# Two transformer blocks in split fp32: activations streamed as 512-wide high-and-low rows in the feed-forward up layers, 512-wide query, key and value chunks, head tiles turned amid a chunk, and bias masks built on GpSimd

## The reference, cut to what matters

```python
# first block, feed-forward of each of 2 layers (D_FF = 2816)
gt, up = jnp.split(h @ w_ffn_in[l], 2, axis=-1)
x = x + (jax.nn.silu(gt) * up) @ w_ffn_out[l]
# second block, feed-forward of each of 2 layers (4096 hidden)
#   x + gate * (relu(h @ mlp_w1)**2 @ mlp_w2)
# dilated attention: bias of a pair of tokens from a table of 32 buckets
bucket = t5_bucket(pk[:, :, None, :] - pq[:, :, :, None])
bias = jnp.moveaxis(bias_table[bucket], -1, 2).astype(jnp.float32)
# first block: q, k, v of 8 heads, width 512 each; q and k normed by head
q, k, v, ... = jnp.split(h @ w_in[l], IN_SPLITS, axis=-1)
```

## Time and profile before

| | us |
|---|---|
| median of 3 runs (1594.33 to 1598.21) | 1595.7 |
| the profiled execution's own time | 1595.42 |
| its span in the trace | 1593.6 |
| TensorE busy with matmuls | 1541.6 |
| VectorE busy | 1127.9 |
| ScalarE busy | 819.0 |
| POOL (GpSimd) busy | 130.7 |

### The profile page before, as it was taken

One profiled execution on the slowest core, in us unless ns is written; L12 is line 12 of the kernel. 1 busy time (PEld: TensorE's weight loads), 2 busy tenths in 40 slices (PEclk: granted clock), 3 DMA queues, 4 the chain that ended last, 5 costly groups with the idle time before them and its releaser, 6 DMA issues. The chain is left out here.

```text
span 1593.6 us, 27186 instructions
## 1 busy us (share of the span) xinstructions
PE 1541.6 (97%) x11270; PEld 1407.5 (88%) x11270; DVE 1127.9 (71%) x1437; ACT 819.0 (51%) x1089; POOL 130.7 (8%) x119
## 2 busy tenths in 40 slices
PE   7999999999999999999998999999999999999998
PEld 7999988999899999999987789998888888889997
DVE  6798668775679757877678666666878766765554
ACT  6564444444555444344468654445555555564442
POOL 2060000000114000000013000000201102000000
PEclk9999999999999999999999999999999999999999
DMA  9775376677676637676732357674877754355652
GB/s 305 256 239 203 128 254 204 214 239 238 224 265 228 196 107 254 226 234 214 232 120 96 95 183 246 220 253 153 306 249 270 245 185 159 121 171 174 196 185 80
DMA packets 231018, 325.44 MB, mean 204 GB/s; under 512 B 7944, under 2 KB 195824, under 8 KB 230896
## 3 DMA queue, kind: packets, MB, share of 16 engines
q1 hardware_dynamic: 223832, 313.00, 58.8%
q10 hardware_dynamic: 7064, 10.71, 2.0%
HBM read 314.23 MB, written 9.45 MB: 203 GB/s over the span
## 5 line engine op out<-in xcount | busy, mean ns | idle before, releaser
L1710 DVE TENSOR_TENSOR wparts<-raw,wparts 128x2048 fp32r<-128x2048 f32 (+1 forms) x240 | 547.1, 2283 | 223.6 <-ACT wparts L1218 223.3
L1218 ACT ACTIVATE wparts<-raw 128x2048 fp32r<-128x2048 f32 (+1 forms) x240 | 454.8, 1896 | 124.5 <-PE bank L555 84.8
L553 PE MATMUL bank<-hT,wparts 128*128 128x256 f32 x1728 | 494.0, 286 | 3.6 <-DVE hT L1831 2.1
L554 PE MATMUL bank<-hT,wparts 128*128 128x256 f32 x1728 | 488.8, 283 | 0.0
L555 PE MATMUL bank<-hT,wparts 128*128 128x256 f32 x1728 | 488.8, 283 | 0.0
L553 PEld LDWEIGHTS bank<-hT,wparts 128*128 128x128 f32 x1728 | 331.1, 192 | 10.3 <-issue 8.1
L554 PEld LDWEIGHTS bank<-hT,wparts 128*128 128x128 f32 x1728 | 331.4, 192 | 1.2
L555 PEld LDWEIGHTS bank<-hT,wparts 128*128 128x128 f32 x1728 | 331.3, 192 | 0.0
L553 PE MATMUL bank<-wparts,hT 128*128 128x256 f32 (+2 forms) x688 | 227.0, 330 | 3.9 <-DVE wparts L1710 2.1
L555 PE MATMUL bank<-wparts,hT 128*128 128x256 f32 (+2 forms) x688 | 222.1, 323 | 0.0
L554 PE MATMUL bank<-wparts,hT 128*128 128x256 f32 (+2 forms) x688 | 222.0, 323 | 0.0
(11 more groups left out here) (285 smaller groups left out, 1484.4 us busy)
## 6 DMA issues: line engine op xcount, KB each, us to landing
raw<-in_mlp_w SPq DMA_DIRECT2D x64, 1024.0 KB, 5.8
ada_raw<-in_ada_w SPq DMA_DIRECT2D x96, 512.0 KB, 6.7
raw<-in_w_ffn_in SPq DMA_DIRECT2D x44, 1024.0 KB, 5.3
raw<-in_w_in SPq DMA_DIRECT2D x43, 1024.0 KB, 5.9
raw<-in_dil_w_in SPq DMA_DIRECT2D x64, 512.0 KB, 4.7
raw<-in_w_ffn_out SPq DMA_DIRECT2D x22, 1024.0 KB, 5.1
raw<-in_w_o SPq DMA_DIRECT2D x8, 1024.0 KB, 5.4
biasb<-head_bias ACTq DMA_DIRECT2D x16, 512.0 KB, 5.6
```

Source lines behind the costliest of these rows:

```text
L553: pe.matmul(dst, held[:, 0, :], streamed[:, 0, :], start=start, stop=False)
L554: pe.matmul(dst, held[:, 0, :], streamed[:, 1, :], start=False, stop=False)
L1218: act.activation(view(whi[c % SPL], c), view(raw[c % RAW], c), ACT.Copy).then_inc(s_hi, 1)
L1710: dve.tensor_tensor(view(wlo[c % SPL], c), view(raw[c % RAW], c), view(whi[c % SPL], c).bitcast(F32), ALU.subtract).then_inc(s_lo, 1)
```

## The change

1. `hT` is laid out so that for each k the high and the low row of 256 tokens lie side by side. `hidden_slabs` takes the place of `feature_major` in GT, UP and M1: one matmul of 512 columns gives high x high in the left half of a bank and high x low in the right half, and one of 256 columns adds low x high to the right half. Each block of 128 hidden columns has its own bank, of four. ScalarE copies the right half to SBUF, VectorE adds it to the left half. SiLU, then product (now of two SBUF tiles), and ReLU with square in one instruction follow.
2. Query, key and value chunks hold half of the contraction and all 512 columns, for `wide_half`. Turns, copies and head norms follow tiles of 128 tokens.
3. In the dilated stage the second tile of a group is turned amid a chunk, not behind it; ScalarE's copy of it comes ahead of its other work of the chunk.
4. The steps and masks of the bias units move from VectorE to GpSimd (POOL). A mask is now eight instructions of 102x128, each with a per-partition scalar.

```diff
-        hT, aT = sb("hT", [P, 2, DK, S], F32R), sb("aT", [P, 2, DK, S], F32R)
+        hT_both, aT = sb("hT", [P, DK, 2, S], F32R), sb("aT", [P, 2, DK, S], F32R)
+        hT = hT_both[:, :, :, :].rearrange("p k b s -> p b k s")
...
-                for c in range(2):
-                    chunk((n, l, c), kmajor(w_in, c0 + 256 * c, 256))
+                for half in range(2):
+                    chunk((n, l, half), kmajor(w_in[512 * half:512 * half + 512], c0, DA))
...
+            def hidden_slabs(name, w, first_of=None):
+                bks = {}
+                for t, k, _, _ in block_order(2, DK, first_of):
+                    if t not in bks:
+                        bks[t] = begin("w", name + (t,), b=slab_bank())
+                    await_pair(first_of, t, k)
+                    rows = slice(P * t, P * t + P)
+                    high_and_low = hT_both[:, k, :, :].rearrange("p b s -> p (b s)")
+                    cross = bks[t][:, S:]
+                    if k < DK - 1:
+                        pe.matmul(bks[t][:, :], w[:, 0, k, rows], high_and_low, start=k == 0, stop=False)
+                        pe.matmul(cross, w[:, 1, k, rows], hT[:, 0, k, :], start=False, stop=False)
+                    else:
+                        pe.matmul(cross, w[:, 1, k, rows], hT[:, 0, k, :], start=False, stop=False)
+                        end(pe.matmul(bks[t][:, :], w[:, 0, k, rows], high_and_low, start=False, stop=True), name + (t,))
...
# TensorE, first block
-                    token_major((nm, l, c), w, 0, 256, hT, 0, DK, first_of=None if i else ("nrm", 2 * l))
+                    wide_half((nm, l), (nm, l, half), w, half, None if nm != "Q" else ("nrm", 2 * l),
+                              turn_of(i - 2) if i in (3, 5) else idle)
...
-                            feature_major((nm, l, c), w, (0, P), hT, 0, DK,
-                                          first_of=None if c or i else ("nrm", 2 * l + 1))
+                            hidden_slabs((nm, l, c), w, None if c or i else ("nrm", 2 * l + 1))
...
# TensorE, dilated stage: project
+                if m3 == 1:
+                    wide_half(("DQK", j, g), chunk_name, w, 1, ("nrm", 6) if (j, g) == (0, 0) else None, turn_next)
...
+                elif g == 1:
+                    wide_half(("DV", j), chunk_name, w, 1, between=turn_next)
...
# GpSimd, behind the norm of each feed-forward of the first block
+                pool.wait_ge(s_bits, 2 * (l + 1))
+                link(pool.tensor_copy(hi16[:, :], ihi[:, :]))
...
+                for u in range(NU):
+                    if u >= 4:
+                        full(pool, ("B", l, u - 4))
+                    k0 = unit_keys(l, u)
+                    for i in range(8):
+                        ins = pool.tensor_scalar(Gst[u % 4][:, i, :], relq[:, P * l:P * l + P], relk[:, k0 + i:k0 + i + 1], None,
+                                                 ALU.is_le)
+                    ins.then_inc(s_g, 1)
...
# ScalarE, feed-forward of the first block
+                        act.activation(crf[which == "UP"][:, t, :], bk[:, S:], ACT.Copy).then_inc(s_crossf, 1)
...
# VectorE, feed-forward of the first block
-                        dve.tensor_tensor(h32[c % 2][:, :, :], bk[:, :].rearrange("p (a s) -> p a s", a=2), sg[c % 2][:, :, :],
-                                          ALU.mult).then_inc(drain_sem(nm), 1)
+                        dve.wait_ge(s_silu, NF1 * l + c + 1)
+                        dve.tensor_tensor(h32[c % 2][:, :, :], h32[c % 2][:, :, :], sg[c % 2][:, :, :], ALU.mult)\
+                           .then_inc(s_hid32, 1)
...
+                        dve.tensor_tensor(dst[:, t, :], bk[:, 0:S], crf[which == "UP"][:, t, :], ALU.add).then_inc(drain_sem(nm), 1)
...
-                        dve.tensor_tensor(Gst[u % 4][:, :, :],
-                                          relk[:, k0:k0 + 8].unsqueeze(2).broadcast_to([NR, 8, P]),
-                                          relq[:, P * l:P * l + P].unsqueeze(1).broadcast_to([NR, 8, P]), ALU.is_ge)\
-                           .then_inc(s_g, 1)
```

More of the change, by code:

```diff
@@ L184, in block_pair @@
             sg = [sb(f"sg{i}", [P, 2, S], at=ph) for i in range(2)]
+            crf = [sb(f"crf{i}", [P, 2, S], at=ph) for i in range(2)]
             posb = sb("posb", [96, S], I32, ph)
@@ L229, in block_pair @@
             xnp = sb("xnp", [P, TT, D], at=ph)
-            rl = [sb(f"rl{i}", [P, 2, S], at=ph) for i in range(2)]
+            crm = [sb(f"crm{i}", [P, 2, S], at=ph) for i in range(2)]
             gbc2 = sb("gbc2", [P, D], at=ph)
@@ L807, in _, with gate_rows @@
                         biases(u0 + 3)
[L809 removed]
+            def gate_rows(e, col0, i, place=lambda: None):
                 pe.wait_ge(s_mods, 2 * i + (2 if col0 >= 24 else 1))
                 for half in range(2):
[L812 removed]
+                    bk = begin("w", ("gb", e, half), b=place())
                     for k in range(4):
@@ L1259, in split_half @@
             def split_half(half):
-                rows = slice(DK // 2 * half, DK // 2 * half + DK // 2)
+                rows = slice(2 * half, 2 * half + 2)
                 act.wait_ge((s_half[0], s_raw[0])[half], 16)
@@ new lines, in _ @@
+                split_ahead(("K", l, 1))
+                qk_out(0)
+                squares(2)
+                qk_out(1)
+                squares(3)
+                split_ahead(("V", l, 0))
+                act.wait_ge(s_z, l + 1)
+                link(act.activation(tf[:, :], zf[:, :], ACT.Abs))
+                act.activation(tf[:, :], tf[:, :], ACT.Exp, scale=-1.0).then_inc(s_ac, 1)
+                steps[0] += 1
+                split_ahead(("V", l, 1))
+                qk_out(2)
+                values_out(0)
@@ L1449, in stage_biases, with copy_cross @@
                         act.sem_inc(s_bst, 1)
+                def copy_cross(which, c):
+                    for t in range(2):
+                        bk = full(act, (which, l, c, t))
+                        if c:
+                            emptied(act, (which, l, c - 1, t))
+                        act.activation(crf[which == "UP"][:, t, :], bk[:, S:], ACT.Copy).then_inc(s_crossf, 1)
                 for c in range(NF1 + 1):
@@ new lines, in _ @@
+                begin_tile(3)
+                finish_head_norm()
+                bk = full(dve, ("F", l))
+                dve.tensor_scalar(zf[:, :], bk[0:H1, 0:S], fb[:, l:l + 1], None, ALU.add).then_inc(drain_sem(("F", l)), 1)
+                emptied(dve, ("F", l))
+                link(dve.memset(zero1[:, :], 0.0))
+                dve.tensor_scalar(mf[:, :], zf[:, :], 0.0, None, ALU.min).then_inc(s_z, 1)
+                split_ahead(("V", l, 0))
+                finish_head_norm()
+                split_ahead(("V", l, 1))
@@ L2168, in mlp @@
                     if c < NF2:
-                        nm = ("M1", i, c)
-                        split_ahead(nm)
-                        emptied(dve, nm)
-                        dve.tensor_tensor(h32[c % 2][:, :, :], rl[c % 2][:, :, :], rl[c % 2][:, :, :], ALU.mult)\
-                           .then_inc(s_hid32, 1)
+                        split_ahead(("M1", i, c))
+                        h = h32[c % 2]
+                        for t in range(2):
+                            nm = ("M1", i, c, t)
+                            bk = full(dve, nm)
+                            dve.wait_ge(s_crossm, 2 * (NF2 * i + c) + t + 1)
+                            dve.tensor_tensor(h[:, t, :], bk[:, 0:S], crm[c % 2][:, t, :], ALU.add).then_inc(drain_sem(nm), 1)
+                        for t in range(2):
+                            emptied(dve, ("M1", i, c, t))
+                        dve.scalar_tensor_tensor(out=h[:, :, :], in0=h[:, :, :], scalar=0.0, in1=h[:, :, :], op0=ALU.max,
+                                                 op1=ALU.mult).then_inc(s_hid32, 1)
                         dve.wait_ge(s_hidhi, 2 * NF1 + NF2 * i + c + 1)
```

239 lines of the change are left out of this document (115 added, 124 removed).

## The result

The changed kernel takes 1718.0 us (median of 4 runs, 1712.8 to 1718.4) beside 1596.5 for the kernel before (4 runs of the same session): the ratio is 1.0749, with a 95% interval of 1.0730 to 1.0768. It is 122 us slower. The forecast was 1573, with a range of 1563 to 1607.

The account below looks back on a forecast made before the run. TensorE, busy 97% of the span, was taken as the bound: 1593.6 - 15.7 - 3.7 - 4.9 - 2.7 + 5.1 = 1571.7, plus 1.8 outside the span, gave 1573 us, with a range of 1563 to 1607.

Parts of the forecast that it names:

- Part 6: Masks on POOL, block one's feed-forward: 0.28 us a piece where up to 0.27 keeps pace, costing TensorE 5.1 us.
- debt: TensorE time lost to late POOL masks: 5.1 us for each 0.01 us a piece over the pace.
- the budget: Sharing of a 17.8 us round in block one's feed-forward: VectorE takes 9.8 us, 8.0 are left for POOL.
- the gains of 27 us: Forecast savings from up layers, query/key/value chunks, dilated turns and the first mask wait, before any cost of POOL's masks.
- rival C: POOL bounds block one's feed-forward, kernel slower, above 0.333 us a piece; chance 0.27 beyond 1600.5 us, 0.05 between 1591 and 1600.5.
- Part 4: First mask of the bias units: with steps and masks on POOL, TensorE's two waits go, saving 2.7 us.
- Part 1: Up layers: a 512-wide and a 256-wide matmul replace three 256-wide, 12.9 ns less in each of 1216 blocks, 15.7 us.
- part 5: Added copies and additions for the up layers' right halves: cost nothing, covered by 10.9 us in block two.
- Parts 2 and 3: Wide query, key, value chunks save 3.7 us; earlier turns in the dilated stage remove a 4.9 us wait.

Follow-up runs that it names:

- parts 2 and 3 alone: Changed kernel with up layers as before and steps and masks on VectorE in their old place: 1589.9 us, 0.9966 of the kernel before.
- half of each mask: Changed kernel with four of each mask's eight pieces on POOL, the other four keys on VectorE: 1596.5 us, 1.0007 of the kernel before.

## Why the prediction was wrong

**Part 6, the piece, failed.** "I take 0.28, nearest in kind to the two-input rows", with 0.42 as the upper bound. Measured: 0.60 long and 0.577 apart, over the upper bound. The step behind it, "half of 2.15 for one input in place of two", was wrong in kind: the column rate is 2.5 ns, above the 2.15 of two inputs, and the fixed part 0.28 beside 0.185. The bound from above took a two-input row as the slowest that 128 columns can be, and no row of before held an instruction with a scalar. In its own sum 0.577 gives 30.7 x 5.1 = 157 us of debt and 1725, where 1718 was measured, but that nearness is luck. The masks cost 126 us, not 157, since VectorE kept 7.1 us a round from POOL and not the 9.8 less 0.7 of the budget, 32 us over 16 rounds; and the gains of 27 us that the sum takes off came to 4. VectorE's splits, which were to lengthen by 0.2 us, took 2.31 us beside 2.29 before: nearly all of the exclusion fell on POOL. So rival C held, and its condition, a piece over 0.333, was met; the chances and the end of the range rested on the wrong bound. The Trainium skill, "GPSIMD Engine Reference", section "Engine selection", calls one-input work on GpSimd roughly line-rate; by it the prediction had the piece at an estimated 0.25. The trace does not agree for the form that was needed: 0.528 with a constant, 0.603 with a scalar from SBUF; only the cast, with 0.293, came near. Its advice against moving elementwise work there held.

**Part 4 failed too.** "The wait goes": it became 8.6 us in layer 0 and 8.1 in layer 1. Masks were to begin at 233 and began at 238.46. POOL's 15 steps, put at 11 us, took 16.5 (from 221.91): five of the six on 96x256 took 1.2 to 2.6 us each beside VectorE. The first mask, eight pieces with a split and a modulation row among them, took 7.5 us more, where eight of 0.28 would be 2.2.

**Part 1 was right in kind and too large, and the rest was eaten.** Alternating widths repeat every 0.352 us in the mlp with masks on VectorE, not 0.347: the 512-wide matmul holds 235 ns, not 227, and the 256-wide one 118. The first and the sixth of six wide ones in a row of blocks:

```profile
961.22 0.40 PE L622 MATMUL bank<-hT,wparts 128*128 128x512 f32 x1
961.46 0.28 PE L623 MATMUL bank<-hT,wparts 128*128 128x256 f32 x1
...
962.98 0.40 PE L622 MATMUL bank<-hT,wparts 128*128 128x512 f32 x1
```

962.98 - 961.22 = 1.76, five times 0.352. That is 8.5 ns gained in a block of 0.360, not 12.9; in the mlp stages 256 blocks x 2 x 8.5 ns = 4.4 us, and the table says 4.2. With widths in runs the mlp stages gain 5.7. In the feed-forward of block one 704 x 8.5 ns = 6.0 us ought to come and the stages get 5.4 us longer than with parts 2 and 3 alone (207.3 + 205.5 against 203.9 + 203.5). The account against the kernel with parts 2 and 3 alone: the wait for the first masks is 7.0 us, not 3.4; 2.3 us are waited for the additions of the right halves (`sg`), which hold a bank; and 10.2 us more ran at half clock around those waits, which by the columns that TensorE streamed in it cost an estimated 4.4 us. 3.6 + 2.3 + 4.4 - 6.0 = 4.3 of the 5.4. TensorE comes to unit 0 at the same time after the norm's first turn in both (38.6 and 38.5 us in layer 0), but the mask is there 2.05 us later in layer 0 and 1.8 in layer 1: VectorE has eight additions, 3.0 us, ahead of its steps and masks. So "Cost nothing" (part 5) held in block two, with its cover of 10.9 us, and failed in block one, ahead of the first mask above all.

**Parts 2 and 3 were right in kind, smaller in size**: 1.9 + 1.1 for 3.7, and 3.2 for 4.9, though the wait for the turned tile went whole. The other 1.7 us of the dilated stage fit its clock: over the first 20 us of the stage the mean granted clock was 0.83, and 0.91 in the kernel before, which is 1.6 us. No run changed that alone.

**The half clock** was in no term. It is plain in TensorE's order of time behind a wait of the changed kernel:

```profile
278.92 0.39 PE L558 MATMUL bank<-wparts,aT 128*128 128x512 f32 x1
279.14 0.39 PE L559 MATMUL bank<-wparts,aT 128*128 128x512 f32 x1
279.37 0.39 PE L560 MATMUL bank<-wparts,aT 128*128 128x512 f32 x1
284.16 0.37 PE L820 MATMUL bank<-dsel,Gst 102*128 102x16 bf16 x8 [4.40 <-POOL Gst L1227]
284.38 0.77 PE L558 MATMUL bank<-wparts,aT 128*128 128x512 f32 x1
284.96 0.63 PE L559 MATMUL bank<-wparts,aT 128*128 128x512 f32 x1
285.38 0.63 PE L560 MATMUL bank<-wparts,aT 128*128 128x512 f32 x1
285.81 0.63 PE L558 MATMUL bank<-wparts,aT 128*128 128x512 f32 x1
286.24 0.63 PE L559 MATMUL bank<-wparts,aT 128*128 128x512 f32 x1
286.66 0.63 PE L560 MATMUL bank<-wparts,aT 128*128 128x512 f32 x1
287.09 0.63 PE L558 MATMUL bank<-wparts,aT 128*128 128x512 f32 x1
287.52 0.50 PE L559 MATMUL bank<-wparts,aT 128*128 128x512 f32 x1
287.85 0.40 PE L560 MATMUL bank<-wparts,aT 128*128 128x512 f32 x1
288.08 0.40 PE L558 MATMUL bank<-wparts,aT 128*128 128x512 f32 x1
```

Starts 0.23 apart before the wait are 0.43 apart behind it (1.2 GHz in place of 2.4), and 0.23 again from 287.85. The same in two stretches of the feed-forwards, the clock being the third number from the right:

```profile
core 0: us, PE busy (x) PEld busy (x) DVE busy (x) ACT busy (x) POOL busy (x), PEclk, DMA share, GB/s
200.00:440.00 240.00, 189.12 (x1109) 154.30 (x1110) 118.75 (x127) 95.50 (x130) 217.08 (x266) 0.90 0.50 167
640.00:880.00 240.00, 191.51 (x1166) 158.89 (x1166) 119.01 (x130) 96.23 (x131) 198.47 (x246) 0.92 0.49 168
```

In all 110 us of the changed kernel were at half clock, beside 11 of before. It is not to be added to the debt: POOL has no idle time in its 205 us, so it sets the round, and a slower TensorE only arrives later and waits less. Against the kernel with the masks on VectorE, units 0 to 31 take 198.5 - 140.6 and 197.6 - 140.0 us, together 115.5 us more, and the first unit comes 4.5 and 4.9 us later in its stage. That is 124.9 us, and the two stages differ by 124.6. The granted clock does cost where the wait stands alone, as at the first mask.

## What to carry to other kernels

Before work moves to an engine that has none of its kind in the trace, take the price of that very form (operand kinds included) as unknown upward, not only downward, and measure it first: four instructions at the end of a program told what the forecast needed. Then compare pieces a round, plus the time in which the other engine shuts this one out, with the round of the engine that waits; above that line every piece is paid in full, and just below it only a lead hides the lack, as with half of each mask. And look at what the added work of an engine stands in front of: here 3 us of small additions ahead of the first mask made it 2 us late in each layer.

## What the runs showed of the hardware that was not expected

- On POOL a 102x128 instruction with a scalar takes longer (0.53 us with a constant, 0.60 from SBUF) than one with two tensors (0.40) or a cast (0.29).
- A split of 2.29 us on VectorE cost POOL 2.0 us on average (44.9 us for 23) and a modulation row of 1.28 us 0.7, while VectorE's additions and products that read a PSUM bank cost POOL nothing; VectorE's splits hardly lengthened (2.31 us).
- POOL's own time for four masks was 18.2, 22.0 and 25.6 us with 16, 24 and 32 pieces, more than pieces and a constant part of VectorE make.
- A stop of TensorE of 4.4 us was followed by 3.4 us at 1.2 GHz.
- A 512-wide and a 256-wide fp32r matmul in alternation repeat every 0.352 us (median distances 235 and 118 ns), though runs of each give 227 + 120; with the widths in runs the mlp stages gained 1.5 us more.
